# Value products of two heads in the two column halves of the array, in the first and the third attention

## The reference

```python
# layer 1: 8 heads of 64, 2 key/value groups; three softmax branches with gates, beside an HGRN2 mixer
o = g[..., 0:1] * o_cmp + g[..., 1:2] * o_sel + g[..., 2:3] * o_win
mix = concatenate([o_nsa, o_hgrn]); x = x + mix @ w_out
# layer 2: differential attention, 8 heads with values of 128
# layer 3: 16 heads of 64 share 4 key/value heads; window of 128, a sink in the sum
o = einsum('bnhgqk,bnkhd->bnqhgd', p, vw)      # p: softmax in blocks of 128 queries x 256 keys
x = x + o.reshape(B, S, 1024) @ w_o
```

## Time and profile before

| | |
|---|---|
| median of 3 runs | 1943.61 us (1942.37 to 1944.22) |
| the profiled execution's own time | 1941.7 us |
| its span | 1939.9 us |
| PE, share of the span | 97% |
| PE weight loads | 78% |
| VectorE | 61% |
| ScalarE | 40% |
| POOL | 14% |
| share of the chain that ended last | PE 86%, DVE 9%, ACT 2% |
| L1087 and L1107 in that chain | 1% each |

### The profile page before, as it was taken

The page is one execution under the profiler, slowest core; times in us unless marked ns, Lnnn a source line. Parts: engine busy times, 40 slices in busy tenths (PEclk is TensorE's granted clock), DMA queues, the critical chain, the costliest instruction groups (busy, mean ns, idle before and its releaser), DMA issues.

```text
span 1939.9 us, 24017 instructions
## 1 busy us (share of the span) xinstructions
PE 1890.9 (97%) x9198; PEld 1521.8 (78%) x9198; DVE 1173.7 (61%) x1929; ACT 767.4 (40%) x1644; POOL 268.2 (14%) x212
## 2 busy tenths in 40 slices
PE   7999998999999999999989999999999899999999
PEld 5887777888888888766668888888877788888887
DVE  8466898755354466588765535445977665445453
ACT  4445666332232233366633323223367533223231
POOL 3000342111011021111021101101210011011010
PEclk9999999999999999999989999999999999999999
DMA  5232000233323323322123333332331123333322
GB/s 217 62 98 66 23 1 1 87 94 95 96 96 98 98 87 108 95 81 71 50 76 98 97 94 95 96 97 89 107 97 50 50 87 98 98 98 98 98 92 93
DMA packets 51249, 166.53 MB, mean 86 GB/s; under 512 B 6848, under 2 KB 7232, under 8 KB 50880
## 3 DMA queue, kind: packets, MB, share of 16 engines
q1 hardware_dynamic: 51136, 165.00, 27.5%
HBM read 155.01 MB, written 2.10 MB: 81 GB/s over the span
## 4 chain that ended last, share of the span: by engine, by line
PE 86%; DVE 9%; ACT 2%; issue 2%; DMA 1%; SPq 0%; DVEq 0%; ACTq 0%
PE bank L897 24%; PE bank L899 24%; PE bank L898 24%; PE bank L1007 2%; PE bank L871 2%; PE bank L872 2%; PE bank L873 2%; PE bank L1063 1%; PE bank L920 1%; PE bank L1087 1%; PE bank L1096 1%; DVE HX L1848 1%; PE bank L1107 1%; DVE SM L1686 1%; DVE WL L1471 1%
## 5 line engine op out<-in xcount | busy, mean ns | idle before, releaser
L1191 ACT ACTIVATE WH<-RAW 128x512 fp32r<-128x512 f32 (+2 forms) x584 | 331.0, 613 | 793.3 <-PE bank L899 717.5
L1471 DVE TENSOR_TENSOR WL<-RAW,WH 128x512 fp32r<-128x512 f32 (+2 forms) x584 | 449.9, 804 | 74.1 <-ACT WH L1191 67.7
L897 PE MATMUL bank<-HH,WH 128*128 128x512 f32 x1056 | 425.4, 403 | 18.4 <-DVE WL L1471 9.8
L897 PE MATMUL bank<-GH,WH 128*128 128x512 f32 x1088 | 434.6, 399 | 2.1 <-DVE GL L1746 2.1
L899 PE MATMUL bank<-GH,WL 128*128 128x512 f32 x1088 | 424.5, 390 | 0.0
L898 PE MATMUL bank<-GL,WH 128*128 128x512 f32 x1088 | 424.1, 390 | 0.0
L899 PE MATMUL bank<-HH,WL 128*128 128x512 f32 x1056 | 413.4, 391 | 0.0
L898 PE MATMUL bank<-HL,WH 128*128 128x512 f32 x1056 | 413.0, 391 | 0.0
L897 PEld LDWEIGHTS bank<-HH,WH 128*128 128x128 f32 x1056 | 199.5, 189 | 65.9 <-DVE WL L1471 9.8
L897 PEld LDWEIGHTS bank<-GH,WH 128*128 128x128 f32 x1088 | 204.8, 188 | 46.2 <-issue 2.9
L898 PEld LDWEIGHTS bank<-GL,WH 128*128 128x128 f32 x1088 | 204.9, 188 | 43.1 <-issue 2.9
(11 more groups left out here) (228 smaller groups left out, 1977.3 us busy)
## 6 DMA issues: line engine op xcount, KB each, us to landing
RAW<-in_wgu SPq DMA_DIRECT2D x132, 512.0 KB, 3.5
RAW<-in_wd SPq DMA_DIRECT2D x48, 512.0 KB, 3.5
RAW<-in_wd SPq DMA_DIRECT2D x24, 384.0 KB, 3.1
RAW<-in_da_qk SPq DMA_DIRECT2D x16, 512.0 KB, 3.6
TMP<-TMP SPq DMA_DIRECT2D x104, 64.0 KB, 2.0
RAW<-in_w_inh SPq DMA_DIRECT2D x12, 512.0 KB, 3.5
RAW<-in_w_in SPq DMA_DIRECT2D x8, 512.0 KB, 6.6
RAW<-in_w_out SPq DMA_DIRECT2D x8, 512.0 KB, 3.6
```

Source lines behind the costliest of these rows:

```text
L897: e.matmul(b, w_h, hi[st.x][k], start=(k == 0), stop=False)
L1191: e.activation(whs[s % NW][:, a:b], raw[s % NR][:, a:b], ACT.Copy).then_inc(S["wh"], 1)
L1471: e.tensor_tensor(wls[s % NR][:, a:b], raw[s % NR][:, a:b], whs[s % NW][:, a:b].bitcast(F), ALU.subtract).then_inc(S["wl"], 1)
```

## The change

In the first attention `vl` runs at odd n only, for both heads of the pair. For each block j it issues two matmuls with the same 64 columns of values, one on the even head's weights into partitions 0 to 63 of the bank, the other on the odd head's into partitions 64 to 127. `tc` gets four buffers (`pts_n`, two of them from `tmp`). In the third attention the same is done for the two heads c of a pair, and `vl` runs once per unit of scores, after both copies; `tc` has four buffers there too. `VP` and `VW` lose their zeros: the tile of `VP` shrinks from 6T to 2T, the memsets go, and evictions of values no longer wait for them. The plan's cost for a product of a block stays 230 ns and now stands for both heads. The left-out hunks change the plan's cost of the two POOL steps and lower the value of the semaphore `zeros` from 4 to 3.

```diff
--- before.py
+++ after.py
@@ -361,7 +361,11 @@
             o.add("DVE", ("wt", a, i), (500 + 2 * w if a == "d" else 300 + w), ("ex", a, i), ready(i))
             g = base + i
             o.add("PE", ("tn", a, i), w // 128 * 110, ("wt", a, i), ("tc", *chain[g - 1]) if i else prior)
-            o.add("ACT", ("tc", a, i), 100 + w, ("tn", a, i), ("vl", *chain[g - 2]) if g >= 2 else None)
+            if a == "n":
+                used = ("vl", a, i // 2 * 2 - 3) if i >= 4 else None
+            else:
+                used = ("vl", *chain[g - 2]) if g >= 66 else ("vl", "n", 63)
+            o.add("ACT", ("tc", a, i), 100 + w, ("tn", a, i), used)
             yield i, w
 
 
...
@@ -422,8 +426,9 @@
         return ("qn", "in", 4 + h // 2), ("kt", "in", 2 + b), ("c_smv", 3) if n < 2 else None
     for n, w in softmax("n", 64, lambda n: 128 * (nsa(n)[2] + 1), after_n, ("e_hvv", 2), lambda n: ("e_vgr", nsa(n)[2]),
                         ("c_tpa", 3)):
-        o.add("PE", ("vl", "n", n), w // 128 * 230 + (900 if n % 16 == 0 else 0), ("tc", "n", n), ("e_vgv", 3),
-              n % 16 == 0 and (("nom", n // 16 - 1) if n else ("c_va", 1)))
+        if n % 2:
+            o.add("PE", ("vl", "n", n), w // 128 * 230 + (900 if n % 16 == 1 else 0), ("tc", "n", n), ("e_vgv", 3),
+                  n % 16 == 1 and (("nom", n // 16 - 1) if n > 1 else ("c_va", 1)))
         if n % 16 == 15:
             o.add("ACT", ("nom", n // 16), 500, ("vl", "n", n))
     dense("h3", early=True)
...
@@ -540,14 +545,15 @@
             o.add("DVE", ("mx", "s", s), 850, ("sc", "s", q), ("nsv",))
             o.add("ACT", ("ex", "s", s), 1200, ("mx", "s", s), q >= 2 and ("tn", "s", 2 * q - 3))
         o.add("DVE", ("wt", "s", q), 1700, ("ex", "s", 2 * q + 1))
+        pair = q // 2
         for n in (2 * q, 2 * q + 1):
-            pair, blocks = n // 4, 4 if n % 4 else 2
+            blocks = 4 if n % 4 else 2
             o.add("PE", ("tn", "s", n), 110 * blocks, ("wt", "s", q), ("tc", "s", n - 1) if n else ("e_vsv", 2))
-            o.add("ACT", ("tc", "s", n), 100 + 128 * blocks, ("tn", "s", n), ("vl", *(("s", n - 2) if n >= 2 else ("d", 30 + n))))
-            o.add("PE", ("vl", "s", n), 230 * blocks, ("tc", "s", n), ("e_vsv", 3),
-                  n % 4 == 0 and pair and ("omca", "so", pair - 1))
+            o.add("ACT", ("tc", "s", n), 100 + 128 * blocks, ("tn", "s", n), ("vl", "s", q - 2) if q >= 2 else ("vl", "d", 31))
+        o.add("PE", ("vl", "s", q), 920 if q % 2 else 700, ("tc", "s", 2 * q + 1), ("e_vsv", 3),
+              q % 2 == 0 and pair and ("omca", "so", pair - 1))
         if q % 2:
-            o.add("ACT", ("omca", "so", pair), 500, ("vl", "s", n), pair >= 2 and ("omlv", "so", pair - 2))
+            o.add("ACT", ("omca", "so", pair), 500, ("vl", "s", q), pair >= 2 and ("omlv", "so", pair - 2))
             o.add("ACT", ("omha", "so", pair), 520, ("omca", "so", pair), last[ST["vs"].u0 + 1])
             o.add("DVE", ("omlv", "so", pair), 620, ("omha", "so", pair))
     dense("so")
@@ -657,7 +663,7 @@
 
         ktt = [[p1(2 * b + g, T) for g in range(2)] for b in range(2)]
         qtt = [p1(4 + p, T) for p in range(4)]
-        VP, PTC = p1(8, 6 * T), p1(14, 2 * T)
+        VP, PTC = p1(10, 2 * T), p1(14, 2 * T)
         vp = VP.rearrange("p (i b c) -> p i b c", i=4, b=4)
         OM, HV = p1(16, 4 * T), p1(20, 4 * T)
         w1 = [p1(16, 4 * T), p1(20, 4 * T)]
@@ -675,9 +681,10 @@
 
         qd, kd = [[PX[:, (10 + 2 * s + t) * T:(11 + 2 * s + t) * T] for s in range(4)] for t in range(2)]
         p_n, p_d, p_s = pb[0:4], pb[0:4] + [hx[7], hx[15]], pb[0:4]
-        pts = pb[4:6]
+        pts_n, pts = pb[4:6] + tmp[4:6], pb[4:6]
         kw = PX[:, 0:5 * T].rearrange("p (k t) -> p k t", k=4)
-        VW = PX[:, 10 * T:16 * T].rearrange("p (i k c) -> p i k c", i=4, k=4)
+        VW = PX[:, 10 * T:12 * T].rearrange("p (i k c) -> p i k c", i=4, k=4)
+        pts_s = pb[4:6] + [PX[:, (12 + k) * T:(13 + k) * T] for k in range(2)]
         om3 = [PX[:, (16 + k) * T:(17 + k) * T] for k in range(2)]
         qw = [PX[:, (18 + s) * T:(19 + s) * T] for s in range(4)]
         NS = SM[:, 64:80]
@@ -1069,10 +1076,10 @@
                 pt, cols = pts[g % 2], slice(i * 128, (i + 1) * 128)
                 if a == "n":
                     h, b, i = nsa(n)
-                    if n % 16 == 0:
+                    if n % 16 == 1:
                         p.wait_ge(S["c_vc"], 8)
                         p.wait_ge(S["c_pt"], 4)
-                        if n == 0:
+                        if n == 1:
                             p.wait_ge(S["c_kc"], 2)
                         else:
                             p.wait_ge(S["n_om"], n // 16)
@@ -1082,10 +1089,12 @@
                     p.wait_ge(S["vg_o"], 4)
                     p.wait_ge(S["tc"], g + 1)
                     for j in range(i + 1):
-                        v = vp[:, j, 2 * b + h // 4, :]
-                        v = v[:, 64:192] if h % 2 == 0 else v[:, 0:128]
-                        done = e.matmul(ob[:, cols], v, pt[:, j * 128:(j + 1) * 128], start=False,
-                                        stop=(n % 16 == 15 and j == i), skip_group_check=True)
+                        for c in range(2):
+                            done = e.matmul(ob[64 * c:64 * c + 64, cols], vp[:, j, 2 * b + h // 4, :],
+                                            pts_n[(n - 1 + c) % 4][:, j * 128:(j + 1) * 128], start=False,
+                                            stop=(n % 16 == 15 and j == i), skip_group_check=True)
+                            if j == i and c == 0:
+                                done.then_inc(S["vl"], 1)
                 elif a == "d":
                     hd = n // 4
                     if i == 0:
@@ -1097,16 +1106,18 @@
                                         pt[:, j * 128:(j + 1) * 128], start=(i == 0), stop=(i == 3 and j == 3),
                                         skip_group_check=True)
                 else:
-                    pair, half, i = swa(n)
+                    pair = n // 2
                     p.wait_ge(S["vs_o"], 4)
                     p.wait_ge(S["s_om"], pair)
-                    p.wait_ge(S["tc"], g + 1)
-                    for k, (c, j) in enumerate((c, j) for c in range(2) for j in ((i - 1, i) if i else (0,))):
-                        v = VW[:, j, pair // 2, :]
-                        v = v[:, 64:192] if c == 0 else v[:, 0:128]
-                        done = e.matmul(ob[:, cols], v, pt[:, k * 128:(k + 1) * 128],
-                                        start=(i == 0 and k == 0), stop=(i == 3 and k == 3),
-                                        skip_group_check=True)
+                    p.wait_ge(S["tc"], SP_["s"] + 2 * n + 2)
+                    for i in (2 * (n % 2), 2 * (n % 2) + 1):
+                        blocks = (i - 1, i) if i else (0,)
+                        for k, j in enumerate(blocks):
+                            for c in range(2):
+                                col = (c * len(blocks) + k) * 128
+                                done = e.matmul(ob[64 * c:64 * c + 64, i * 128:(i + 1) * 128], VW[:, j, pair // 2, :],
+                                                pts_s[(2 * n + i % 2) % 4][:, col:col + 128], start=(i == 0),
+                                                stop=(i == 3 and k == 1), skip_group_check=True)
                 done.then_inc(S["vl"], 1)
 
             def base(h):
...
@@ -1337,16 +1348,23 @@
                 g = SP_[a] + n
                 w = 128 * (nsa(n)[2] + 1) if a == "n" else 128 * (n % 4 + 1) if a == "d" else 512 if n % 4 else 256
                 p.wait_ge(S["tp"], g + 1)
-                if g >= 2:
+                if a == "n":
+                    p.wait_ge(S["vl"], g // 2 * 2 - 2)
+                    pt = pts_n[n % 4]
+                elif a == "d":
                     p.wait_ge(S["vl"], g - 1)
-                e.activation(pts[g % 2][:, 0:w], ptb[:, 0:w], ACT.Copy).then_inc(S["tc"], 1)
+                    pt = pts[n % 2]
+                else:
+                    p.wait_ge(S["vl"], 96 + max(n // 2 - 1, 0))
+                    pt = pts_s[n % 4]
+                e.activation(pt[:, 0:w], ptb[:, 0:w], ACT.Copy).then_inc(S["tc"], 1)
 
             def nom(k):
                 p.wait_ge(S["vl"], 16 * (k + 1))
                 e.activation(OM[:, k * T:(k + 1) * T], ob, ACT.Copy).then_inc(S["n_om"], 1)
 
             def omc(st, pair):
-                p.wait_ge(S["vl"], SP_["s"] + 4 * (pair + 1))
+                p.wait_ge(S["vl"], SP_["s"] + 2 * (pair + 1))
                 if pair >= 2:
                     p.wait_ge(S["op"], OP["h8"] + pair - 1)
                 e.activation(om3[pair % 2], ob, ACT.Copy).then_inc(S["s_om"], 1)
@@ -1602,9 +1620,8 @@
             def e_vg(i):
                 b, r_ = token_rows("vg", i, 1)
                 g = GT[:, i * 24:(i + 1) * 24]
-                p.wait_ge(S["zeros"], 4)
```

(9 more changed lines are left out.)

10 lines of the change are left out of this document (5 added, 5 removed).

## The result

The changed kernel takes 1927.31 us (median of 4 runs, 1926.12 to 1928.73), the kernel before, run beside it, 1943.91 us (1942.37 to 1944.40): ratio 0.9916, interval 0.9899 to 0.9933. It is 16.6 us faster.

The account below looks back on a forecast made before the run. The PE was taken to bound both attentions, except VectorE in the first's middle. Path gains of 2.7 and 3.9 us, less 0.6 for the plan: 1941.7 - 6.6 + 0.6 = 1935.7 us profiled, 1937.6 median; range 1931 to 1948.

Parts of the forecast that it names:

- Record spacing, 0.111 us, and pairs in the time of one record: Value products in both attentions: records start 0.111 us apart, and a pair of column halves also takes 0.111 us.
- 0.35 us per group for entering and leaving: Each group of half-width value products, in both attentions, pays 0.35 us for changing the array's mode.
- The PE's saving, 7.4 and 6.9 us: PE time saved on value products after mode changes: 7.4 us in the first attention, 6.9 in the third.
- The share on the path, 36% and 57%: Part of the value products' time on the last-ending chain: 12.9 of 35.5 us first attention, 14.1 of 24.9 third.
- The end of the third attention: The last sixteen value records, 2.01 us long, would take 1.1 to 1.3 us.
- Memsets removed, "nothing": The two POOL memsets, 2.83 and 1.85 us, end long before their values are used; removing them gains nothing.
- Plan misjudges, 0.6 us: The plan takes each group for 0.35 us too short; charged 0.6 us, with bounds 0 and 3 us.
- Halves in turn: Rival: a pair's column halves in both attentions don't overlap, so nothing is saved; 1951 us, chance 0.15.
- VectorE takes over, or partial overlap: Rival: VectorE becomes the bound in the attentions, or pairs overlap partly; at most 3 us gained, 1940.6 us, chance 0.2.
- More is won: Rival: mode changes fall into waits or beside masked scores and long runs take all; 11 us, 1932.5 us, chance 0.12.
- The clock: Rival: more PE waiting at the third attention's end brings 1.2 GHz; up to 5 us more, 1942.6 us, chance 0.06.
- The plan's order comes out worse: Rival: the plan's order loses more than the gain, by 17 us of misjudged time; 1946 us, chance 0.05.

Follow-up runs that it names:

- halves_mid: grouped_full with the 64-column halves only in units 16 to 55 of the first attention; 1938.08 us, 0.9982 of the kernel before.
- halves_edge: grouped_full with the 64-column halves only in units 0 to 15 and 56 to 63 of the first attention; 1937.64 us, 0.9972 of the kernel before.
- grouped_full: The changed kernel's groups, buffers and order, but padded values and products of 128 columns; 1937.64 us, 0.9972 of the kernel before.
- one_half: The changed kernel with both heads' products put into partitions 0 to 63, so no two can overlap; 1946.67 us, 1.0018 of the kernel before.
- halves_alone: The kernel before with 64-column products, each into its own head's half, in the old groups; 1948.09 us, 1.0024 of the kernel before.
- plan_cost: The changed kernel with the plan's cost of each product group raised by 350 ns; 1930.97 us, 0.9938 of the kernel before.
- again: The changed kernel once more, with no edit; 1926.83 us, 0.9924 of the kernel before.
- memset_back: The changed kernel with a 128x3072 memset on POOL, and the value evictions' wait for it, put back; 1930.01 us, 0.9930 of the kernel before.
- n_only: The kernel before with the change in the first attention only; 1934.95 us, 0.9964 of the kernel before.
- in_turn: The changed kernel issuing all products of one half of a group, then all of the other; 1931.40 us, 0.9939 of the kernel before.

## Why the prediction was wrong, point by point

**What bounds the kernel** was read rightly: PE, VectorE, PE in the first attention, PE in the third, by the earlier trace rows. halves_mid, halves_edge and the two clock losses bear it out.

**Record spacing, 0.111 us, and pairs in the time of one record**: right. Within a group pairs follow 0.109 us apart, and sixteen records take 1.09 us, against the 1.08 of the row pairs in the earlier trace rows, on which the choice of 0.111 over 0.222 rested. The Trainium skill, TensorE: Matmul & The Clock Gate, Part 3 (What overlaps and what doesn't), lets a load overlap only matmuls of another row group; here both halves use all rows, and the trace doesn't agree: 16 records in 1.09 us, each with a load of 0.137 us that begins beneath the running matmuls.

**0.35 us per group for entering and leaving**: about right where a group stands between full-width matmuls. By the formula halves lose 0.13 us with four records and gain 0.54 with sixteen; measured against grouped_full it is 0.13 lost and 0.61 gained.

**The PE's saving, 7.4 and 6.9 us**: too small, measured 10.1 and 8.7. The term left out the other part of the change. It counted groups of before as records alone (0.444 per block) and halved nothing but the records; that before has 96 groups and after 48, and that each full-width group also costs something beyond its records, wasn't in it. grouped_full shows that part by itself: PE busy 0.65 us less in the first attention (202.93 against 203.58) and in the third 2.2 less (160.14 against 162.29):

```profile
1402.37:1570.72 168.35, 160.14 (x889) 125.28 (x896) 121.21 (x223) 95.94 (x271) 19.54 (x15) 0.99 0.24 69
```

And groups beside L1014, the masked scores, which change the mode anyway, save more: eight records cost 0.26 us less than in grouped_full there, against 0.15 between full ones. The halves alone, after against grouped_full, save 9.5 and 6.5 us of PE time, so for the third attention 6.9 was close and what it lacked is the grouping's 2.2. With the shares on record, 10.1 and 8.7 us would have made 3.6 + 4.9 = 8.6 instead of 6.6. This is the smaller part of the miss.

**The share on the path, 36% and 57%**: this step failed. It multiplied the saving by the line's part in the chain that ended last. That chain is one route. In a stretch where the PE is busy for 54.5 of 55 us, a piece of the chain that runs through VectorE's normalisation or ScalarE's exponential doesn't mean that the PE was free: it worked on other things meanwhile, and had as much to do. Nearly every microsecond of the PE counts there, whether its line is named in the chain or not: in the third attention 84% where 57% had been taken.

In the first attention the 36% are two things, nothing for the middle and, outside it, 12.9 of the 15.3 us of the other 138 records, 84%. Outside the forecast was near: 93% of the PE's 4.2 us came out, 3.9 us. What failed there is "nothing" for the middle, which became 2.3 us shorter (108.76 to 106.44), half of it by grouping and buffers alone. The forecast's sign that this stretch keeps its length didn't come. Runs give the shares, as stage time over PE busy time:

| comparison | first attention | third attention |
|---|---|---|
| after against before | 6.2 of 10.1, 61% | 7.3 of 8.7, 84% |
| after against grouped_full | 4.7 of 9.5, 49% | 6.2 of 6.5, 95% |
| after against one_half | 10.1 of 15.6, 65% | 9.3 of 10.2, 91% |
| halves_alone against before | 6.3 of 11.4, 55% | |
| edges alone, middle alone | 3.0 of 3.6, 4.6 gave 0.8 | |

The chain's 36% and 57% lie below every row of after. In the third attention after lost 1.7 us more to 1.2 GHz than before, grouped_full and one_half, so its shares there are if anything too low. What the window view of the earlier trace rows would have given (182 records in the VectorE-bound stretch, so 138 of 320, or 43%, outside) is nearer for the first attention; for the third it says nearly all. That chain shares mislead because the route is one among several equal ones is my reading of these numbers; the numbers themselves are measured.

**The end of the third attention**: the sixteen records of the earlier trace rows (2.01 us) are now these, and `so` starts 3.18 us after their start instead of 4.08, as forecast (1.1 to 1.3 us for the run):

```profile
1520.65 1.09 PE L1118 MATMUL bank<-PX 128*64 128x128 f32 x16 [0.69 <-ACT PX L1360]
1523.83 0.50 PE L904 MATMUL bank<-GH,WH 128*128 128x512 f32 x1 [2.09 <-DVE GL L1763]
```

**Memsets removed, "nothing"**: wrong by 1.5 to 2.0 us, by the first of the two. The step asked when the zeros are used, which is late, and not what runs beside the memset. The Trainium skill, SBUF — State Buffer, Who interferes with whom, says that a VectorE tensor_scalar can take the pair of ports that it shares with GpSimd, and that the one that starts second then waits for the whole of the other; the trace agrees, with 2.18 us beside the memset and 0.48 without.

**Plan misjudges, 0.6 us**: no such loss was seen; with the price told (plan_cost) the kernel is not faster.

**The rivals.** *Halves in turn*: excluded; one_half shows what it would have cost, 1946.67 us, where 1951 was put. *VectorE takes over, or partial overlap*: the overlap is full, and VectorE leads the chain only in what is left. *More is won* (1932.5 us, chance 0.12): this is what came, and by still more. Its reasoning, that long runs take all and changes of mode fall beside L1014, was half of it; its number kept the chain's shares and so ended too high. *The clock*: it came in part. Around the end of the third attention the clock is lower than before, windows of 45 us, before and after:

```profile
1505.00:1550.00 45.00, 39.45 (x221) 31.09 (x220) 27.66 (x52) 24.85 (x70) 3.28 (x3) 0.96 0.15 43
```

```profile
1505.00:1550.00 45.00, 39.25 (x199) 30.33 (x200) 28.31 (x44) 19.20 (x47) 5.87 (x5) 0.92 0.20 60
```

0.96 is 1.8 us of the full rate lost, 0.92 is 3.6. again and memset_back have 0.92 in that window too. In all eight profiles whose third attention runs its halves side by side, the stage lost 3.4 or 5.1 us of full rate; of the six others four, before among them, lost 1.7, and two (n_only and halves_edge, with full-width products there) 3.4. So the loss seems to come with the change, but also without it, and how much of the 1.8 us is the change's own stays open. *The plan's order comes out worse*: no.

**The sum again**, with what after's trace shows: start 1.5, first attention 6.2, third 7.3, together 15.0 us that belong to the change; `do` another 3.2 and the rest back 2.4 (both mostly clock). That makes 15.7 us, which rounded spans show as 15.8. On record stood 0, 2.7 and 3.9, less 0.6 for the plan. The range was too narrow at its lower end, because it took 11 us as the most that could be won when the PE's own saving was uncertain by a third and the share by half and more.

## What to carry to other kernels

Where an engine is busy for nearly the whole of a stretch, price what you take from it nearly in full (82 to 95% came out here), whatever share the chain gives to the line. Where another engine is the bound, less of it comes out (2.3 of 6.0 us here, in part with that engine's own busy time), but don't put it at nothing. Two products of up to 64 output rows belong into the two column halves of the array, issued alternately and in groups of at least eight records, for between full-width matmuls a group of four lost 0.13 us here. Before calling a removed instruction free, look at what the neighbouring engines' instructions lasted while it ran.

## What the runs showed of the hardware that I had not expected

Matmuls of the two column halves needn't be issued alternately to overlap: with eight of one half ahead of eight of the other (in_turn), the second half began while three of the first were still to start, and groups of up to eight records lost 0.05 us at most. The order costs 0.48 us in a group of sixteen (1.92 against 1.44).

Entering and leaving the half-width mode costs a group of sixteen 0.25 us more than the same records at full width (one_half against grouped_full).

A memset of 128x3072 on POOL held an independent VectorE instruction of 0.48 us for 1.7 us more, in each of the seven kernels that have it.

After similar waits of the PE, executions of the same code there differ in the granted clock: 0.94 (after) and 0.77 (memset_back) over the same 30 us after the second attention, which moves a stage by 3 us and, in a single profile, looks like an effect of whatever was changed.
